# Two expert passes of at most 128 tokens with the tokens stationary and the weights streamed

## Chip, cores and metric

One core of one Trainium2 chip runs the whole program. The metric is the device time of one execution in microseconds (us). Three runs of the kernel before gave 4410.6, 4415.4 and 4421.4 us, median 4415.4 us.

## What is computed

A two-layer backbone over 1024 tokens of width 1024 (float32). The change is in the last large part, the mixture of experts of the second layer. Each token goes to 2 of 8 experts:

```python
def _moe_swiglu(h, w_router, w_gate, w_up, w_down):
    ...
    top_val, top_idx = lax.top_k(logits, TOP_K)
    ...
    g = lax.ragged_dot(xs, w_gate, group_sizes)
    u = lax.ragged_dot(xs, w_up, group_sizes)
    y = lax.ragged_dot(jax.nn.silu(g) * u, w_down, group_sizes)
    y = y * weights.reshape(-1)[order][:, None].astype(y.dtype)
    out = jax.ops.segment_sum(y, token_of, num_segments=n)
```

and the layer adds `mx[5] * _moe_swiglu(...)` to its stream, where `mx[5]` is a vector of 1024 numbers, the layer's gate. Gate and up weights are 1024 x 3584 per expert, down weights 3584 x 1024. How many tokens an expert gets is known only on the chip.

## The kernel before

The tokens of an expert are packed into passes of at most 512 (`TOKENS`). There are nine passes in this input. A table on the chip holds each pass's expert and its width class, one of `WIDTHS` (128, 160, 256, 288, ... 512). Every engine reads that table and branches to code for that width (`each_width`). So a pass of at most 128 tokens runs `one_pass(p, 128, True)`.

A pass walks over `C` = 14 chunks of 256 hidden features (`CHUNK_FF`). Float32 products are made from two fp32r parts each: a rounded part ("hi") and the rest ("lo"), with the products hi x hi, hi x lo and lo x hi. Per chunk:

- SP loads 1 MB of gate, 1 MB of up and 1 MB of down weights, into one buffer each (`raw_g`, `raw_u`, `raw_d`). A buffer is loaded again once its rest has been formed. SP's order is gate, up, down of the chunk before (`load_in`, L1807 and L1810; `load_down`, L1816).
- ACT (ScalarE) rounds each to its hi tile (`round_up`, L1985). DVE (VectorE) forms the rest of gate and up (`rest`, L2100). POOL (GpSimd) forms the rest of down (`rest_d`, L1847). Hi and lo tiles are double, one for even and one for odd chunks.
- PE (TensorE) has weights stationary and tokens moving. In a narrow pass (128 or 160 tokens) hi and lo tokens lie side by side as one moving operand of 256 or 320 columns (`product`, L1894 and L1895). `hidden` makes 32 products a chunk (2 blocks of 128 features, gate and up, 8 blocks of the input width), `down` makes 16, each of two matmuls: 96 matmuls a chunk.
- DVE adds the two halves of each sum (L2109). ACT applies SiLU (L2010). DVE multiplies by up (L2133), ACT rounds (L2017), DVE forms the rest (L2140). That gives the moving operand of `down`.
- `down` writes each of 8 blocks of the output width to one of four banks. DVE scales by the gate column and adds it to a sum in SBUF (L2149, L2153), and PE waits for a bank to be read (`y_added`) before it writes it again.

PE's order in step c is hidden(c), then down(c-1). At the end of a pass the sum is turned by PE (L1953), copied (L2056, L2221) and stored (L2060). The tokens of the next pass are turned by PE (L1883), scaled and rounded by ACT (L2029, L2032) and split by DVE (L2159) before the next pass's first `hidden`. With the last `down`, the turns of the next tokens are placed ahead of its wait for the rest of the weights. ACT's `Silu` and its `Copy` at the head of a loop body come with a table load (`ACT_TABLE_LOAD`) in every second chunk, since loop bodies hold two chunks (`chunk_pairs`).

A vector of the modulation is summed in `modulation_rest_phase`. It makes each vector in `rows` by two ones-matmuls (L851): four vectors, of which three are stored in memory. Those in `columns` are made as columns (L855). The dense layer (`ffn`) uses the same `expert_mlp_phase` at 512 tokens, with no table.

Of the kernel before, what the change touches and what calls it, by code (L numbers as in the profile page):

```python
# [792 lines left out]
def modulation_rest_phase(nc, b_ada, w_out, dram, keep):  # L793
# [7 lines left out]
    with ctx:  # L801
# [5 lines left out]
        rows = [i for i, (layer, vec) in enumerate(REST_VECTORS) if vec < 3]  # L807
# [838 lines left out]
def expert_mlp_phase(nc, name, shape, weights, columns, ident, rows_of, y_rows, table, prepare=None):  # L1646
# [590 lines left out]
def backbone(nc, a, tables, out):  # L2237
    F, R, I = mybir.dt.float32, mybir.dt.float32r, mybir.dt.int32
    dram = dict(tables)
    for name, shape, dtype in (("pool_mod", [3, D], F), ("x1", [SEQ, D], F), ("x3", [SEQ, D], F), ("xn", [SEQ, D], F),  # L2240
                               ("y_dense", [SEQ, D], F), ("y", [SLOT_TILES * P, D], F), ("slot_token", [LISTED_TILES * P, 1], I)):
        dram[name] = nc.dram_tensor(f"scratch_{name}", shape, dtype).ap()
    outer = ExitStack()
    with outer:
# [69 lines left out]
        def slot_tile(pool, p, t, to):  # L2314
# [37 lines left out]
```

## Time and profile before

| | |
|---|---|
| median of 3 runs | 4415.4 us |
| the profiled execution | 4412.7 us |
| its span (first to last instruction) | 4410.9 us |
| PE busy | 3861.9 us (88%) |
| DVE busy | 2323.4 us (53%) |
| ACT busy | 1755.2 us (40%) |
| POOL busy | 826.3 us (19%) |
| instructions | 65249 |
| mean granted TensorE clock | 0.933 of full |

Busy shares are over the whole span, and the expert part alone is about 2600 us of it, from 1784 us on. What the change is worth has to be read in the stretches of the passes that it touches.

### The profile page before, as it was taken

The numbers are of one execution on the slowest core, as the hardware profiler recorded it, in microseconds if no ns is written. First come the engines' busy times: TensorE is split into PE (matmuls) and PEld (weight loads), VectorE is DVE, ScalarE is ACT, GpSimd is POOL, SyncE is SP. The second block draws the span as 40 slices with busy tenths as digits, with TensorE's granted clock in tenths as the row PEclk, the third lists the DMA queues.
The fourth block names the chain that finished last, engine by engine and source line by source line (L and its number), as shares of the span: only waits on it lengthen the run. The fifth ranks groups of instructions, "written<-read, shape, count | busy, mean of one in ns | idle before, by whom it ended". The sixth has DMA issues, their size and how long they took to land. (4 is left out here: it accounts for less than half of the span.)

```text
span 4410.9 us, 65249 instructions
## 1 busy us (share of the span) xinstructions
PE 3861.9 (88%) x23414; PEld 3521.9 (80%) x23415; DVE 2323.4 (53%) x3372; ACT 1755.2 (40%) x2324; POOL 826.3 (19%) x319
## 2 busy tenths in 40 slices
PE   5998867999999762698999989988899998998993
PEld 3974445877877651688999989988899998998993
DVE  2338733454545452586654444448654487544555
ACT  5146613322322131555443333335533355443443
POOL 0000001111111121332222122213221233222222
PEclk8989878999999986899999999999999999999997
DMA  5136634323332233675553434346544366444554
GB/s 169 38 125 240 229 94 172 105 95 95 105 95 86 78 132 90 201 232 183 185 169 133 143 132 149 126 144 231 196 144 143 129 219 210 156 149 146 175 167 186
DMA packets 433192, 661.23 MB, mean 150 GB/s; under 512 B 33361, under 2 KB 348881, under 8 KB 432977
## 3 DMA queue, kind: packets, MB, share of 16 engines
q1 hardware_dynamic: 413026, 587.84, 40.0%
q0 software_dynamic: 15776, 55.61, 3.6%
q10 hardware_dynamic: 4176, 15.21, 0.9%
q8 instruction: 100, 1.64, 0.2%
q14 instruction: 114, 0.93, 0.1%
HBM read 599.32 MB, written 59.29 MB: 149 GB/s over the span
## 5 line engine op out<-in xcount | busy, mean ns | idle before, releaser
L1847 POOL TENSOR_TENSOR moe_d_lo<-moe_raw_d,moe_d_hi 128x2048 fp32r<-128x2048 f32 x126 | 582.8, 4625 | 1823.0 <-ACT moe_d_hi L1985 1823.0
L2153 DVE SCALAR_TENSOR_TENSOR moe_y_t<-moe_y,moe_cols,moe_y_t 128x256 f32<-128x256 f32 (+3 forms) x936 | 482.2, 534 | 185.5 <-PE moe_y L1898 176.9
L1896 PE MATMUL moe_g<-moe_x,moe_g_hi 128*128 128x352 f32 (+3 forms) x1344 | 421.2, 313 | 36.6 <-issue 36.3
L2100 DVE TENSOR_TENSOR moe_g_lo<-moe_raw_g,moe_g_hi 128x2048 fp32r<-128x2048 f32 x127 | 360.9, 2842 | 135.6 <-ACT moe_g_hi L1985 134.3
L1897 PE MATMUL moe_g<-moe_x,moe_g_hi 128*128 128x352 f32 (+3 forms) x1344 | 420.6, 313 | 0.0
L1896 PE MATMUL moe_y<-moe_h,moe_d_hi 128*128 128x352 f32 (+3 forms) x1344 | 417.9, 311 | 2.1 <-DVE moe_y_t L2153 1.1
L1898 PE MATMUL moe_g<-moe_x,moe_g_lo 128*128 128x352 f32 (+3 forms) x1344 | 419.2, 312 | 0.0
L1897 PE MATMUL moe_u<-moe_x,moe_u_hi 128*128 128x352 f32 (+3 forms) x1344 | 416.1, 310 | 0.0
L1897 PE MATMUL moe_y<-moe_h,moe_d_hi 128*128 128x352 f32 (+3 forms) x1344 | 416.0, 310 | 0.0
L1896 PE MATMUL moe_u<-moe_x,moe_u_hi 128*128 128x352 f32 (+3 forms) x1344 | 415.3, 309 | 0.0
L1898 PE MATMUL moe_u<-moe_x,moe_u_lo 128*128 128x352 f32 (+3 forms) x1344 | 415.0, 309 | 0.0
L1898 PE MATMUL moe_y<-moe_h,moe_d_lo 128*128 128x352 f32 (+3 forms) x1344 | 414.9, 309 | 0.0
L2133 DVE TENSOR_TENSOR moe_h_full<-moe_h_full,moe_u 128x352 f32<-128x352 f32 (+3 forms) x168 | 81.8, 487 | 582.2 <-PE moe_u L1898 582.1
L2017 ACT ACTIVATE moe_h<-moe_h_full 128x352 fp32r<-128x352 f32 (+5 forms) x252 | 106.0, 421 | 640.6 <-DVE moe_h_full L2133 640.6
L2100 DVE TENSOR_TENSOR moe_u_lo<-moe_raw_u,moe_u_hi 128x2048 fp32r<-128x2048 f32 x127 | 290.1, 2285 | 9.1 <-ACT moe_u_hi L1985 9.1
L1896 PEld LDWEIGHTS moe_g<-moe_x,moe_g_hi 128*128 128x128 f32 x1344 | 257.4, 191 | 38.9 <-issue 38.3
L2010 ACT ACTIVATE moe_h_full<-moe_g 128x352 f32<-128x352 f32 (+3 forms) x168 | 73.2, 436 | 526.8 <-PE moe_g L1898 526.7
L1898 PEld LDWEIGHTS moe_g<-moe_x,moe_g_lo 128*128 128x128 f32 x1344 | 258.2, 192 | 0.0
L1897 PEld LDWEIGHTS moe_g<-moe_x,moe_g_hi 128*128 128x128 f32 x1344 | 257.7, 192 | 0.0
L1985 ACT ACTIVATE moe_g_hi<-moe_raw_g 128x2048 fp32r<-128x2048 f32 x127 | 242.2, 1907 | 38.9 <-DMA moe_raw_g<-in_moe_w_gate 38.2
L1896 PEld LDWEIGHTS moe_y<-moe_h,moe_d_hi 128*128 128x128 f32 x1344 | 253.1, 188 | 3.4 <-DVE moe_y_t L2153 2.4
L1898 PEld LDWEIGHTS moe_u<-moe_x,moe_u_lo 128*128 128x128 f32 x1344 | 254.3, 189 | 0.0
(317 smaller groups left out, 9504.4 us busy)
## 6 DMA issues: line engine op xcount, KB each, us to landing
moe_raw_g<-in_moe_w_gate SPq DMA_DIRECT2D x127, 1024.0 KB, 5.6
moe_raw_u<-in_moe_w_up SPq DMA_DIRECT2D x127, 1024.0 KB, 5.0
moe_raw_d<-in_moe_w_down SPq DMA_DIRECT2D x126, 1024.0 KB, 4.9
att_w_mod<-in_w_ada SPq DMA_DIRECT2D x20, 2048.0 KB, 8.5
scratch_y<-att_zeros SPq DMA_DIRECT2D x11, 2048.0 KB, 13.8
ffn_raw_g<-in_ffn_w_gate SPq DMA_DIRECT2D x22, 1024.0 KB, 5.4
ffn_raw_u<-in_ffn_w_up SPq DMA_DIRECT2D x22, 1024.0 KB, 5.4
ffn_raw_d<-in_ffn_w_down SPq DMA_DIRECT2D x22, 1024.0 KB, 4.8
```

The source lines that it names most:

```text
L1847: pool.tensor_tensor(d_lo[par][:, :, :], raw_d[:, :, :], d_hi[par][:, :, :].bitcast(F), ALU.subtract)\
L1896: pe.matmul(bank[:, 0:width], wh, moving[:, 0, 0:width], start=start, stop=False)
L1897: pe.matmul(bank[:, 0:width], wh, moving[:, 1, 0:width], start=False, stop=False)
L1898: return pe.matmul(bank[:, 0:width], wl, moving[:, 0, 0:width], start=False, stop=stop)
L1985: act.activation(hi[par][:, :, :], raw[:, :, :], ACT.Copy).then_inc(rounded, 1)
L2010: act.activation(h_full[:, f, 0:width], gate, ACT.Silu).then_inc(silu_done, 1)
L2017: act.activation(h[par][:, f, 0, 0:width], h_full[:, f, 0:width], ACT.Copy).then_inc(h_rounded, 1)
L2100: dve.tensor_tensor(lo[par][:, :, :], raw[:, :, :], hi[par][:, :, :].bitcast(F), ALU.subtract).then_inc(split, 1)
L2133: dve.tensor_tensor(h_full[:, f, 0:width], h_full[:, f, 0:width], up, ALU.mult)\
L2153: dve.scalar_tensor_tensor(y_t[:, db, 0:cols], y_ps[db % 4][:, 0:cols], gate, y_t[:, db, 0:cols], ALU.mult, ALU.add).then_inc(y_added, 1)
```

## The change

For a pass of width class 128 of the expert part, and for no other, each engine now runs `pass_of_few` in place of the old body. Loads (SP), `rest_d` (POOL) and the formulas of rounding and rest stay. New in it:

- Gate and up tiles share one tile, `gu_hi` and `gu_lo`, side by side. For every pass, wide ones too, they are now written and read as 8 runs of 256 with a stride of 512.
- `hidden_few`: the tokens (128 x 128 block, hi or lo) are the stationary operand, gate and up weights stream as 512 columns. Three matmuls for each of 8 blocks of the input: 24 a chunk, into one bank.
- `silu_few`, `whole_few`: one SiLU and one product a chunk, 256 wide, in place of two of each and four sums of halves.
- `turn_few`: the result has tokens on partitions, so PE turns it back (2 transposes), between the two halves of the next chunk's `hidden_few`. ACT rounds what is turned (`round_few`), DVE forms the rest (`rest_few`).
- `down_few`: the turned hidden block is stationary, down weights stream as 512 columns: 12 matmuls a chunk, summed in two banks over all 14 chunks. The 8 sums a chunk on DVE are gone.
- At the end two multiplies by the gate as a row, and one store. The gate row comes from memory by a DMA that ACT issues at the pass's start. `modulation_rest_phase` makes that vector as a fourth stored row as well as a column. The turn of the result is gone.
- In the last chunk the turns of the next tokens come behind the wait for the rest of the down weights, where they stood ahead of it.

ACT's order in a step is: round gate (c+1), SiLU (c), round up (c+1), round hidden (c), round down (c). DVE's is: rest of gate (c+1), product (c), rest of up (c+1), rest of hidden (c).

```diff
-        rows = [i for i, (layer, vec) in enumerate(REST_VECTORS) if vec < 3]
+        rows = [i for i, (layer, vec) in enumerate(REST_VECTORS) if vec < 3 or (layer, vec) == (1, 5)]
...
+        gu_hi = [sb(f"gu_hi{i}", [P, KD, 2, CHUNK_FF], R) for i in range(2)]
+        gu_lo = [sb(f"gu_lo{i}", [P, KD, 2, CHUNK_FF], R) for i in range(2)]
+        g_hi, u_hi = ([w[:, :, side, :] for w in gu_hi] for side in range(2))
+        g_lo, u_lo = ([w[:, :, side, :] for w in gu_lo] for side in range(2))
...
+            def hidden_few(p, c, par, first, count):
+                n = p * C + c
+                early = type(c) is int and c < 2
+                if first == 0:
+                    if early and c == 0:
+                        pe.wait_ge(x_split, (p + 1) * KD + 2)
+                    pe.wait_ge(g_split, n + W0 + 1)
+                    pe.wait_ge(u_split, n + W0 + 1)
+                    if not early:
+                        pe.wait_ge(h_whole, (n - 1) * FB + H0)
+                for k in range(first, first + count):
+                    wh, wl = (w[par][:, k, :, :].rearrange("p s f -> p (s f)") for w in (gu_hi, gu_lo))
+                    bank = g_ps[par][:, :]
+                    pe.matmul(bank, x[:, k, 0, 0:P], wh, start=(k == 0), stop=False)
+                    pe.matmul(bank, x[:, k, 0, 0:P], wl, start=False, stop=False)
+                    last = pe.matmul(bank, x[:, k, 1, 0:P], wh, start=False, stop=(k == KD - 1))
+                if first + count == KD:
+                    last.then_inc(u_done, FB)
+
+            def turn_few(p, c, par):
+                n = p * C + c
+                pe.wait_ge(h_whole, (n + 1) * FB + H0)
+                if not (type(c) is int and c == 0):
+                    pe.wait_ge(h_split, (n - 1) * FB + H0)
+                for f in range(FB):
+                    last = pe.transpose(u_ps[par][:, f * P:(f + 1) * P], h_full[:, par, f * P:(f + 1) * P], ident[:, :])
+                last.then_inc(g_done, FB)
+
+            def down_few(p, c, par):
+                n = p * C + c
+                first, final = (type(c) is int and c == at for at in (0, C - 1))
+                if first:
+                    pe.wait_ge(y_left, p * TILES_PASS + O0)
+                    pe.wait_ge(y_right, p * TILES_PASS + O0)
+                pe.wait_ge(d_split, n + W0 + 1)
+                pe.wait_ge(h_split, (n + 1) * FB + H0)
+                if final:
+                    for k in range(4):
+                        turn_rows(p + 1, k)
+                for half in range(2):
+                    cols = slice(half * 512, (half + 1) * 512)
+                    for f in range(FB):
+                        if final:
+                            turn_rows(p + 1, 4 + half * FB + f)
+                        hh, hl = (h[par][:, f, i, 0:P] for i in range(2))
+                        pe.matmul(y_ps[half][:, :], hh, d_hi[par][:, f, cols], start=first and f == 0, stop=False)
+                        pe.matmul(y_ps[half][:, :], hh, d_lo[par][:, f, cols], start=False, stop=False)
+                        last = pe.matmul(y_ps[half][:, :], hl, d_hi[par][:, f, cols], start=False, stop=final and f == FB - 1)
+                last.then_inc(y_done, KD)
+
+            def pass_of_few(p):
+                def step(c, par):
+                    hidden_few(p, c, par, 0, KD // 2)
+                    turn_few(p, c - 1, 1 - par)
+                    hidden_few(p, c, par, KD // 2, KD // 2)
+                    down_few(p, c - 1, 1 - par)
...
+            def pass_of_few(p):
+                act.wait_ge(y_turned, p * KD + T0)
+                act.dma_start(gate_all, gate_row.partition_broadcast(P)).then_inc(gate_loaded, 16)
+
+                def step(c, par):
+                    round_g(p, c + 1, 1 - par)
+                    silu_few(p, c, par)
+                    round_u(p, c + 1, 1 - par)
+                    round_few(p, c, par)
+                    round_d(p, c, par)
...
+                def step(c, par):
+                    rest_g(p, c + 1, 1 - par)
+                    whole_few(p, c, par)
+                    rest_u(p, c + 1, 1 - par)
+                    rest_few(p, c, par)
...
+                for half in range(2):
+                    cols = slice(half * 512, (half + 1) * 512)
+                    last = dve.tensor_tensor(y_out[:, 0, cols], y_ps[half][:, :], gate_all[:, cols], ALU.mult)
+                last.then_inc(y_right, TILES_PASS)
```

## Rows read from the trace of the kernel before

**Rows 1.** The page's busy times, then its slices (tenths of full clock).

```profile
PE 3861.9 (88%) x23414; PEld 3521.9 (80%) x23415; DVE 2323.4 (53%) x3372; ACT 1755.2 (40%) x2324; POOL 826.3 (19%) x319
...
PEclk8989878999999986899999999999999999999997
```

**Rows 2.** Groups by line and shape, 1780 to 4411 us: busy, mean ns | idle before.

```profile
L1894 PE MATMUL moe_g<-moe_x,moe_g_hi 128*128 128x256 f32 x448 | 115.5, 293 | 13.8 <-DVE moe_x L2159 6.2 <-issue 5.7 <-DVE moe_g_lo L2100 1.9
```

**Rows 3.** Timeline of PE in one narrow chunk: start, duration in us [idle before].

```profile
1890.88 0.58 PE L1894 MATMUL moe_y<-moe_h,moe_d_hi 128*128 128x256 f32 x1 [1.89 <-DVE moe_y_t L2153]
...
1891.47 0.41 PE L1894 MATMUL moe_y<-moe_h,moe_d_hi 128*128 128x256 f32 x1
1891.68 0.41 PE L1895 MATMUL moe_y<-moe_h,moe_d_lo 128*128 128x256 f32 x1
...
1894.40 0.28 PE L1894 MATMUL moe_g<-moe_x,moe_g_hi 128*128 128x256 f32 x1
1894.52 0.28 PE L1895 MATMUL moe_g<-moe_x,moe_g_lo 128*128 128x256 f32 x1
```

**Rows 4.** Stretches: us, busy (x) of PE, PEld, DVE, ACT, POOL, PEclk, DMA share, GB/s.

```profile
1879.20:1906.40 27.20, 24.98 (x193) 24.58 (x192) 22.02 (x37) 15.93 (x17) 9.12 (x3) 0.94 0.70 233
...
1890.90:1894.30 3.40, 3.40 (x16) 3.40 (x17) 2.64 (x7) 2.44 (x2) 1.77 (x1) 0.50 0.95 317
1796.60:1802.20 5.60, 5.59 (x26) 5.60 (x27) 1.78 (x2) 5.34 (x5) 2.12 (x3) 0.50 0.73 226
```

**Rows 5.** Timeline of POOL at both ends of the two narrow passes of 128.

```profile
1810.98 4.60 POOL L1847 TENSOR_TENSOR moe_d_lo<-moe_raw_d,moe_d_hi 128x2048 fp32r<-128x2048 f32 x1 [10.51 <-ACT moe_d_hi L1985]
...
1974.45 4.62 POOL L1847 TENSOR_TENSOR moe_d_lo<-moe_raw_d,moe_d_hi 128x2048 fp32r<-128x2048 f32 x1 [8.97 <-ACT moe_d_hi L1985]
1988.06 4.54 POOL L1847 TENSOR_TENSOR moe_d_lo<-moe_raw_d,moe_d_hi 128x2048 fp32r<-128x2048 f32 x1 [9.00 <-ACT moe_d_hi L1985]
...
2977.25 4.59 POOL L1847 TENSOR_TENSOR moe_d_lo<-moe_raw_d,moe_d_hi 128x2048 fp32r<-128x2048 f32 x1 [26.05 <-ACT moe_d_hi L1985]
...
3141.22 4.60 POOL L1847 TENSOR_TENSOR moe_d_lo<-moe_raw_d,moe_d_hi 128x2048 fp32r<-128x2048 f32 x1 [8.98 <-ACT moe_d_hi L1985]
```

**Rows 6.** Timeline of POOL, then of DVE, in the pass that follows the first.

```profile
2028.69 4.65 POOL L1847 TENSOR_TENSOR moe_d_lo<-moe_raw_d,moe_d_hi 128x2048 fp32r<-128x2048 f32 x1 [21.46 <-ACT moe_d_hi L1985]
...
2030.45 5.04 DVE L2100 TENSOR_TENSOR moe_g_lo<-moe_raw_g,moe_g_hi 128x2048 fp32r<-128x2048 f32 x1 [3.19 <-ACT moe_g_hi L1985]
2035.41 0.41 DVE L2133 TENSOR_TENSOR moe_h_full<-moe_h_full,moe_u 128x256 f32<-128x256 f32 x1
2035.74 2.28 DVE L2100 TENSOR_TENSOR moe_u_lo<-moe_raw_u,moe_u_hi 128x2048 fp32r<-128x2048 f32 x1
```

**Rows 7.** Timeline of ACT: a narrow chunk, a wide one, a narrow pass's start.

```profile
1890.33 0.31 ACT L2017 ACTIVATE moe_h<-moe_h_full 128x128 fp32r<-128x128 f32 x1 [3.14 <-DVE moe_h_full L2133]
1890.55 1.90 ACT L1985 ACTIVATE moe_d_hi<-moe_raw_d 128x2048 fp32r<-128x2048 f32 x1
...
2023.27 0.40 ACT L2017 ACTIVATE moe_h<-moe_h_full 128x256 fp32r<-128x256 f32 x1
...
2964.85 1.28 ACT L1985 ACT_TABLE_LOAD   x1 [6.08 <-PE moe_u L1895]
```

**Rows 8.** Timeline of PE: 512 columns in the dense layer, and transposes.

```profile
900.04 0.39 PE L1896 MATMUL ffn_g<-ffn_x,ffn_g_hi 128*128 128x512 f32 x1
900.27 0.39 PE L1897 MATMUL ffn_g<-ffn_x,ffn_g_hi 128*128 128x512 f32 x1
...
1988.34 0.60 PE L1883 MATMUL moe_g<-ident,moe_x_rows 128*128 128x128 f32 x4
```

**Rows 9.** The page's DMA issues: count, KB each, median us to landing.

```profile
moe_raw_d<-in_moe_w_down SPq DMA_DIRECT2D x126, 1024.0 KB, 4.9
```

**Rows 10.** Timeline of PE in the modulation's rest: the ones-matmuls, rows then columns.

```profile
574.24 10.07 PE L851 MATMUL rest_row_ps<-mod_sum,rest_ones 128*128 128x512 f32 x16 [15.59 <-DMA rest_col_bias<-in_b_ada]
584.15 17.86 PE L855 MATMUL rest_col_ps<-rest_ones,mod_sum 128*128 128x1 f32 x96
```

More of the change, by code:

```diff
@@ L1643, in _, with expert_mlp_phase @@
                 norm(t)
-def expert_mlp_phase(nc, name, shape, weights, columns, ident, rows_of, y_rows, table, prepare=None):
+def expert_mlp_phase(nc, name, shape, weights, columns, ident, rows_of, y_rows, table, prepare=None, gate_row=None):
     F, R = mybir.dt.float32, mybir.dt.float32r
@@ L1714, in expert_mlp_phase, with few @@
         y_done, y_added, y_turned, y_left, y_right = (sem(n) for n in ("y_mm", "y_add", "y_t2", "y_l", "y_r"))
+        gate_loaded = sem("gate_ld") if table is not None else None
+        gate_all = y_t[:, 0:2, :].rearrange("p a b -> p (a b)")
+        def few(width):
+            return table is not None and width == P
         W0, U0, X0, H0, Y0, A0, T0, O0 = 1, 2 * FB, KD, FB, 2 * KD, 4, KD, TILES_PASS
@@ L1958, in one_pass @@
             def one_pass(p, width, narrow):
+                if few(width):
+                    pass_of_few(p)
+                    return
                 hidden(p, 0, parity(p, 0), width, narrow)
@@ L2032, in ready_tokens, with silu_few, round_few @@
                     act.activation(x[:, k, 0, :], x_full[:, k % 2, :], ACT.Copy).then_inc(x_rounded, 1)
-            def one_pass(p, width, narrow):
+            def silu_few(p, c, par):
+                act.wait_ge(u_done, (p * C + c + 1) * FB + U0)
+                act.activation(h_full[:, par, 0:CHUNK_FF], g_ps[par][:, 0:CHUNK_FF], ACT.Silu).then_inc(silu_done, FB)
+            def round_few(p, c, par):
+                n = p * C + c
+                act.wait_ge(g_done, (n + 1) * FB)
+                act.wait_ge(y_done, (n - 1) * KD + Y0)
+                act.activation(h[par][:, :, 0, 0:P], u_ps[par][:, 0:CHUNK_FF].rearrange("p (f q) -> p f q", f=FB), ACT.Copy)\
+                   .then_inc(h_rounded, FB)
+            def pass_of_few(p):
[7 more added lines that the diff above has]
+                    round_d(p, c, par)
+                chunk_pairs(act, p, 0, C - 2, step)
+                step(C - 1, parity(p, C - 1))
+                ready_tokens(p + 1)
+                act.wait_ge(y_right, (p + 1) * TILES_PASS + O0)
+                act.sem_inc(y_left, TILES_PASS)
+                act.dma_start(y_rows(p, 0), y_out[:, 0, :]).then_inc(y_stored[0], 16)
+                for t in range(1, TILES_PASS):
+                    act.wait_ge(y_stored[t % 2], (p * (TILES_PASS // 2) + t // 2 + 1) * 16)
+                    act.sem_inc(y_stored[t % 2], 16)
+            def one_pass(p, width, narrow):
+                if few(width):
+                    pass_of_few(p)
+                    return
+                if table is not None:
+                    act.sem_inc(gate_loaded, 16)
                 def step(c, par, round_next=True):
@@ L2322, in backbone @@
         expert_mlp_phase(nc, "moe", (MAX_PASSES, FF_EXPERT // CHUNK_FF), experts, keep["moe_cols"], keep["ident"], slot_tile,
-                         tile_rows(dram["y"]), keep["table"], list_slots)
+                         tile_rows(dram["y"]), keep["table"], list_slots, dram["pool_mod"][3, :])
         output_phase(nc, a["final_gain"], dram, keep, out)
```

34 lines of the change are left out of this document (29 added, 5 removed).

## The prediction

> **What bounds the kernel now.** The page first: PE is busy 88% of the span and its granted clock is mostly full [rows 1]. That is an average, so the second view is the groups by shape. The 256-column form of L1894 stands 448 times for gate, and a pass makes 14 x 16 = 224 of them, so two of the nine passes have width 128 and take the new code. Everything below is about these two and about their neighbours.
>
> Third, the beat of such a pass, read where POOL starts on each chunk's down weights. From chunk 0 to chunk 12 it is 1974.45 - 1810.98 = 163.5 us in the first and 3141.22 - 2977.25 = 164.0 us in the second, mean 163.7, which is 13.64 us a chunk [rows 5]. PE's own work is less: 96 matmuls, 0.12 us from start to start [rows 3], are 11.5 us. The rest is a stall of 1.89 us in `down`, where PE waits for DVE's sum into `y_t` [rows 3], and a stretch at half clock behind it: two chunks have a mean clock of 0.94, the 3.4 us behind the stall 0.50 [rows 4]. DVE has 22.0 us of work in 27.2, ACT 15.9, POOL 9.1, and the DMA share is 0.70 [rows 4]. So the pass is bound by PE and DVE together, and the others are not far off. The engine that gets faster here is PE. The question is what the order of the other engines allows.
>
> **PE's work.** 512 columns take 0.227 us from start to start (900.04 to 900.27) [rows 8]. 24 + 12 matmuls are 8.2 us, two transposes 0.3: 8.5 us against 11.5. Taken alone that is 3 us a chunk. DVE loses eight sums and four halvings. Neither sets the end, if a loop of waits is longer.
>
> **The loop of waits.** In the new order PE turns hidden block c in the middle of hidden(c+1). From there everything hangs in one chain back to the next turn. Counted from the start of turn(c):
>
> - two transposes: four last 0.60 with 0.11 between starts, so two last 0.38 [rows 8];
> - ACT rounds the turned block: 0.03 to start, 0.40 [rows 7];
> - ACT rounds the down weights right behind, 1.90, with a start 0.09 before the last one's end (1890.55 against 1890.64) [rows 7];
> - POOL forms their rest: 0.08 to start, 4.6 [rows 5];
> - meanwhile ACT rounds gate(c+2), and DVE is to form its rest. Both inputs of that lie in SBUF, as POOL's do. The trace has the case: POOL ran 2028.69 to 2033.34, DVE started L2100 at 2030.45 and took 5.04 instead of 2.28. It ended 2.15 after POOL did, so it hardly moved while POOL ran [rows 6]. In the new order POOL always starts ahead of it, 1.9 us of gate rounding before. So the rest of gate ends 2.15 after POOL;
> - product(c+1), behind it on DVE: 0.41, of which 0.33 adds (2035.41 to 2035.74) [rows 6];
> - rest of up(c+2): 2.28, of which 2.20 adds [rows 6]. ACT has the rounding of up ready by then, even with the two table loads of 1.28 [rows 7] of every second chunk: 0.72 + 1.8 + 1.28 + 1.9 + 1.28 + 0.4 + 1.85 = 9.2 us against the 9.8 at which DVE gets to it;
> - PE starts hidden(c+2) some 0.1 later, and 12 matmuls, 2.72 us, bring it to turn(c+1).
>
> Sum: 0.38 + 0.43 + 1.81 + 4.70 + 2.15 + 0.33 + 2.20 + 0.10 + 2.72 = 14.8 us. That is more than the 13.64 of now. `down`(c) stands on a side branch. It starts 0.2 behind POOL's end, at 7.5, and has until 12.1.
>
> **The clock.** PE is idle from the end of hidden(c+1), about 3.1, to 7.5. After the 1.89 us stall the trace has 3.4 us at 1.2 GHz [rows 3, 4], where 256 columns take 0.21 us [rows 3] and 512 so twice that, 0.427. After 6.2 us of idling before a pass [rows 2] the first 5.6 us were at that level [rows 4]. The low stretch will fall on `down`: 8 matmuls at 0.427 and 4 at 0.227 are 4.3 us, which ends at 11.8 and costs nothing. If it lasts 5.6, `down` ends at 12.7 and 1 us of hidden's half is slow: 1.1 us more. I take 0.25, nearer the 3.4 that repeats in the pass, and so 15.05 us a chunk. Ends for the range: 14.8 and 15.9.
>
> A rule of the Trainium skill speaks against the change here: "TensorE: Matmul & The Clock Gate", section "HAM oscillation — how this bites in real kernels", tells of a product of 128 rows whose bursts between waits each start at the low clock, and advises loops that keep PE fed. By it each chunk pays for one burst. By my chain that burst is `down` and costs 0 to 0.25 us; were every burst slow, it would be the third rival's time. The trace of before agrees in kind: one 1.89 us gap in two chunks is followed by 3.4 us at 0.50 [rows 3, 4].
>
> **The ends of a pass.** The first chunk has no overlap. Before, POOL ended chunk 0 at 1815.6. Now hidden(0) from 1796.6 has 5.6 us at half clock [rows 4], 13 matmuls, and 11 at full: to 1804.6 and 0.2 to drain. SiLU 0.4, up 1.8, rest 2.3: 1809.3. Half of hidden(1), slow at first, 4.3; turn, block, down weights, POOL 0.4 + 0.4 + 1.9 + 4.7: 1821.0, 5.4 us later. In the second pass ACT starts at 2964.85 [rows 7], plus 0.4 for issuing the gate row (a DMA issue; no row has this one, bounds 0 to 1): 1.3 + 1.9 + 1.3 + 0.4 + 1.8 + 2.3 brings rest of up to 2974.3, then the same 4.3 + 7.4 to 2986.0, against 2977.25 + 4.6 = 2981.85: 4.2 later. Mean 4.8.
> Chunk 12 to 13 took 1988.06 - 1974.45 = 13.6 [rows 5]. Now `down`(12) 0.2 + 4.3, turn(13) 0.4, block 0.4, down weights 1.8, POOL 4.7: 11.8, so -1.8.
> Hand-over to the next pass: the turns of its tokens start behind POOL and not before it, up to 4.6 later, but the sums, the turn of the result and its copies go. I take 0, between -3 and +4.
>
> **Around it.** The fourth stored row costs two ones-matmuls of 512 columns. Four records a vector, 10.07 / 16 each, are 2.5 us, and the columns' matmuls follow without a gap [rows 10], so PE ends that phase later by it: +2.5, with 0.1 for one more load. Strided hi and lo tiles change no count of elements: 0, bounds -1 and +8 us over all passes; the wide passes are bound by PE and would hide it. The gate row is read 13 chunks after it is asked for: 0. Removed instructions of PE's sequencer: 0.
>
> **The sum.** Per pass 4.8 + (12 x 15.05 - 163.7) - 1.8 + 0 = 4.8 + 16.9 - 1.8 = 19.9. Two passes 39.8, with 2.6 for the row: +42.4. The profiled execution took 4412.7, so 4455.1. The median of the three runs stands 2.7 above it: 4458, rounded to 4457. What a measurement can tell from no change is 0.3%, 13 us.
>
> **Rivals.**
> 1. The beat falls to the loop of the down buffer, and the kernel gets faster. POOL's end, 0.2 to the DMA issue, 4.9 to land [rows 9], 1.9 + 0.1 on ACT, 4.6 on POOL: 11.7, say 12.0. This needs ACT, DVE and PE never to wait for each other in the order above. 12 x 12.0 - 163.7 = -19.7; with 4.8 - 1.8, -16.7 a pass, -31 in all: 4384. It decides from a beat below 13.3 us, where the ends and the row are paid (24 x 0.36 = 8.6). For it: the 0.70 DMA share leaves room. Against it: the turn in mid-chunk ties ACT's down rounding to PE.
> 2. DVE isn't held by POOL. Then the rest of gate is done by 7, and the chain runs over ACT alone or over `down`. In chunks with table loads 0.38 + 0.43 + 1.8 + 1.3 + 1.9 + 1.3 + 0.4 + 1.85 + 2.28 + 0.1 + 2.72 = 14.5. In the others POOL, `down` and half of hidden: 0.4 + 0.4 + 1.8 + 4.7 + 0.2 + 2.7 to 4.3 + 2.7 = 12.9 to 14.5. Mean about 14.1: 12 x 14.1 - 163.7 = +5.5, +8.5 a pass, +20 in all: 4435. For it: DVE's sums with a PSUM input aren't slowed in the trace. Against it: the 5.04 us row.
> 3. The clock stays low in every burst. `down` 12 x 0.427 = 5.1 and half of hidden 5.1: 0.5 + 0.4 + 1.8 + 4.7 + 0.2 + 5.1 + 5.1 = 17.8. 12 x 17.8 - 163.7 = +49.9, +53 a pass, +109 in all: 4524. For it: PE is to be busy 8.5 of 15 us. Against it: in the pass now the clock came back within 3.4 us each time, with the same kind of gap.
> 4. The new code isn't taken. Excluded by the 448 [rows 2].
>
> **How the numbers follow.** Forecast (beat 14.8 to 15.9, ends and strides within their bounds, 4440 to 4485) 0.72; first rival 0.07; second 0.11; third 0.10. The range of 4424 to 4495 takes in the second rival and the half of the third's way in which part of hidden's half is slow. Slower by over 0.3% is the forecast, the third and nearly all of the second: 0.88. Within 0.3%: the ends between the second and the first, 0.07. Faster: 0.05.
>
> **What the profile will show.** Starts of POOL's L1847 some 15 us apart in two passes. DVE's rest of gate at 3.6 to 5 us there, ending 2.1 after POOL. PE waiting for POOL before `down` by over 3 us each chunk, then slow matmuls in `down` and full ones in hidden. The 512-column matmuls 0.227 apart. PE's busy time lower by some 70 us, and the time longer for all that. The prediction is wrong if the beat is under 13.6, if rest of gate runs at 2.3 us, or if the wide passes change their beat.

## The result and the profile after

The changed kernel took 4468.4 us (median of 4 runs, 4462.6 to 4473.1), the kernel before 4418.4 us beside it. The ratio is 1.0113, with an interval of 1.0089 to 1.0136: slower by 50 us. The forecast was 4457 us with a range of 4424 to 4495. The profiled execution took 4465.0 us, with a span of 4463.2 us against 4410.9.

Of the page of after, the line of busy times, the granted clock in 40 slices, and the group of DVE's rests of gate:

```profile
PE 3830.9 (86%) x21778; PEld 3415.4 (77%) x21779; DVE 2206.2 (49%) x2982; ACT 1738.8 (39%) x2266; POOL 823.6 (18%) x319
PEclk8988878999999986789999999998799999999996
L2217 DVE TENSOR_TENSOR moe_gu_lo<-moe_raw_g,moe_gu_hi 128x2048 fp32r<-128x2048 f32 x127 | 388.9, 3063 | 222.1 <-ACT moe_gu_hi L2062 220.8
```

Every engine has less to do than in [rows 1], and the time is longer. A slice is 111.6 us. In slices 17 and 18 (1785 to 2008 us) the clock is 7 and 8 where the kernel before has 8 and 9, in slices 28 and 29 (3013 to 3236 us) 8 and 7 where it has 9 and 9: the two narrow passes. The page can say no more than that.

POOL's starts on the down weights, from the timeline of after (start, duration, instruction, idle time before it and what ended it), chunks 0, 1, 12 and 13 of the first narrow pass:

```profile
1830.56 4.51 POOL L1854 TENSOR_TENSOR moe_d_lo<-moe_raw_d,moe_d_hi 128x2048 fp32r<-128x2048 f32 x1 [16.48 <-ACT moe_d_hi L2062]
1846.02 4.50 POOL L1854 TENSOR_TENSOR moe_d_lo<-moe_raw_d,moe_d_hi 128x2048 fp32r<-128x2048 f32 x1 [10.95 <-ACT moe_d_hi L2062]
...
2014.49 4.52 POOL L1854 TENSOR_TENSOR moe_d_lo<-moe_raw_d,moe_d_hi 128x2048 fp32r<-128x2048 f32 x1 [10.62 <-ACT moe_d_hi L2062]
2027.32 4.49 POOL L1854 TENSOR_TENSOR moe_d_lo<-moe_raw_d,moe_d_hi 128x2048 fp32r<-128x2048 f32 x1 [8.31 <-ACT moe_d_hi L2062]
```

(2014.49 - 1830.56) / 12 is 15.33 us a chunk. The second narrow pass gives 15.31 in the same way. Before it was 13.64 [rows 5]. From chunk 12 to 13 it is 12.8 us here and 11.8 in the other pass, where before it was 13.6.

Two chunks out of the middle of that pass, from the timeline of after, all engines, in the order of the chain and not of time:

```profile
1904.44 0.38 PE L1992 MATMUL moe_u<-ident,moe_h_full 128*128 128x128 f32 x2
1904.99 0.39 ACT L2121 ACTIVATE moe_h<-moe_u 128x256 fp32r<-128x256 f32 x1 [9.51 <-PE moe_u L1992]
1905.27 1.91 ACT L2062 ACTIVATE moe_d_hi<-moe_raw_d 128x2048 fp32r<-128x2048 f32 x1
1907.26 4.50 POOL L1854 TENSOR_TENSOR moe_d_lo<-moe_raw_d,moe_d_hi 128x2048 fp32r<-128x2048 f32 x1 [11.04 <-ACT moe_d_hi L2062]
1910.43 3.48 DVE L2217 TENSOR_TENSOR moe_gu_lo<-moe_raw_g,moe_gu_hi 128x2048 fp32r<-128x2048 f32 x1 [4.40 <-ACT moe_gu_hi L2062]
1913.84 0.41 DVE L2284 TENSOR_TENSOR moe_h_full<-moe_h_full,moe_g 128x256 f32<-128x256 f32 x1
1914.17 2.28 DVE L2217 TENSOR_TENSOR moe_gu_lo<-moe_raw_u,moe_gu_hi 128x2048 fp32r<-128x2048 f32 x1
1911.82 0.63 PE L2013 MATMUL moe_y<-moe_d_hi,moe_h 128*128 128x512 f32 x1 [4.22 <-POOL moe_d_lo L1854]
...
1915.57 0.40 PE L2013 MATMUL moe_y<-moe_d_hi,moe_h 128*128 128x512 f32 x1
1916.69 0.50 PE L1979 MATMUL moe_g<-moe_gu_hi,moe_x 128*128 128x512 f32 x1 [0.26 <-DVE moe_gu_lo L2217]
1919.57 0.38 PE L1992 MATMUL moe_u<-ident,moe_h_full 128*128 128x128 f32 x2
...
1922.41 4.52 POOL L1854 TENSOR_TENSOR moe_d_lo<-moe_raw_d,moe_d_hi 128x2048 fp32r<-128x2048 f32 x1 [10.65 <-ACT moe_d_hi L2062]
1926.98 0.80 PE L2013 MATMUL moe_y<-moe_d_hi,moe_h 128*128 128x512 f32 x1 [4.25 <-POOL moe_d_lo L1854]
...
1931.84 0.63 PE L2015 MATMUL moe_y<-moe_d_hi,moe_h 128*128 128x512 f32 x1
1932.27 0.51 PE L1979 MATMUL moe_g<-moe_gu_hi,moe_x 128*128 128x512 f32 x1
1935.15 0.38 PE L1992 MATMUL moe_u<-ident,moe_h_full 128*128 128x128 f32 x2
```

What to see: the turn of the hidden block at 1904.44 leads to the block's rounding, the rounding of down, POOL, then DVE's rest of gate. That ends at 1913.91, 2.15 after POOL's end (1911.76), although POOL's work has nothing to do with it. Product, rest of up, half of `hidden`, and the next turn at 1919.57: 15.13 us. In the second chunk rest of up would have let `hidden` go earlier. But all 12 matmuls of `down` run at the low level of TensorE's clock (0.43 from start to start, 1926.98 to 1932.27; the granted clock there is 0.50), and PE gets to `hidden` late: 15.58 us from turn to turn. The two alternate through the pass.

Where the 52.3 us of span went, from the two traces:

| stretch | before | after | difference |
|---|---|---|---|
| start to last matmul of attention | 558.7 | 569.5 | +10.8 |
| from there to the last matmul of the routing (the added row lies here) | 1160.5 | 1161.1 | +0.6 |
| from there to the first matmul of the expert part | 64.4 | 66.6 | +2.2 |
| first to last matmul of the expert part | 2559.3 | 2599.1 | +39.8 |
| from there to the end | 68.0 | 66.9 | -1.1 |

The fourth row was forecast as +39.8. The first has the same code in both kernels, and is treated below.

### The profile page after: what moved, and what is told of

Same layout as the page of the kernel before. It is cut to its first block and busy times, and to the rows that moved or that the text cites. A ratio compares the mean times of both kernels' runs of the same rounds, so it can differ in the third digit from the quotient of the medians.

```text
span 4463.2 us, 60571 instructions
## 1 busy us (share of the span) xinstructions
PE 3830.9 (86%) x21778; PEld 3415.4 (77%) x21779; DVE 2206.2 (49%) x2982; ACT 1738.8 (39%) x2266; POOL 823.6 (18%) x319
## 5 line engine op out<-in xcount | busy, mean ns | idle before, releaser
L2217 DVE TENSOR_TENSOR moe_gu_lo<-moe_raw_g,moe_gu_hi 128x2048 fp32r<-128x2048 f32 x127 | 388.9, 3063 | 222.1 <-ACT moe_gu_hi L2062 220.8
L2270 DVE SCALAR_TENSOR_TENSOR moe_y_t<-moe_y,moe_cols,moe_y_t 128x352 f32<-128x352 f32 (+3 forms) x728 | 392.5, 549 | 176.8 <-PE moe_y L1905 176.1
L1903 PE MATMUL moe_g<-moe_x,moe_gu_hi 128*128 128x352 f32 (+3 forms) x1344 | 421.5, 314 | 35.7 <-issue 25.4
L1904 PE MATMUL moe_g<-moe_x,moe_gu_hi 128*128 128x352 f32 (+3 forms) x1344 | 420.4, 313 | 0.0
L1905 PE MATMUL moe_g<-moe_x,moe_gu_lo 128*128 128x352 f32 (+3 forms) x1344 | 420.3, 313 | 0.0
L1905 PE MATMUL moe_u<-moe_x,moe_gu_lo 128*128 128x352 f32 (+3 forms) x1344 | 415.7, 309 | 0.0
L1903 PE MATMUL moe_u<-moe_x,moe_gu_hi 128*128 128x352 f32 (+3 forms) x1344 | 415.3, 309 | 0.3 <-DVE moe_gu_lo L2217 0.3
L1904 PE MATMUL moe_u<-moe_x,moe_gu_hi 128*128 128x352 f32 (+3 forms) x1344 | 415.3, 309 | 0.0
L2217 DVE TENSOR_TENSOR moe_gu_lo<-moe_raw_u,moe_gu_hi 128x2048 fp32r<-128x2048 f32 x127 | 290.0, 2283 | 13.9 <-ACT moe_gu_hi L2062 13.9
L1903 PEld LDWEIGHTS moe_g<-moe_x,moe_gu_hi 128*128 128x128 f32 x1344 | 258.6, 192 | 38.1 <-issue 36.7
L1904 PEld LDWEIGHTS moe_g<-moe_x,moe_gu_hi 128*128 128x128 f32 x1344 | 258.2, 192 | 0.0
L1905 PEld LDWEIGHTS moe_g<-moe_x,moe_gu_lo 128*128 128x128 f32 x1344 | 258.0, 192 | 0.0
L1903 PEld LDWEIGHTS moe_u<-moe_x,moe_gu_hi 128*128 128x128 f32 x1344 | 253.9, 189 | 0.5 <-DVE moe_gu_lo L2217 0.5
## 6 DMA issues: line engine op xcount, KB each, us to landing
scratch_y<-att_zeros SPq DMA_DIRECT2D x11, 2048.0 KB, 13.6
```

What stands on the lines that cost most here:

```text
L1903: pe.matmul(bank[:, 0:width], wh, moving[:, 0, 0:width], start=start, stop=False)
L1904: pe.matmul(bank[:, 0:width], wh, moving[:, 1, 0:width], start=False, stop=False)
L1905: return pe.matmul(bank[:, 0:width], wl, moving[:, 0, 0:width], start=False, stop=stop)
L2217: dve.tensor_tensor(lo[par][:, :, :], raw[:, :, :], hi[par][:, :, :].bitcast(F), ALU.subtract).then_inc(split, 1)
L2270: dve.scalar_tensor_tensor(y_t[:, db, 0:cols], y_ps[db % 4][:, 0:cols], gate, y_t[:, db, 0:cols], ALU.mult, ALU.add).then_inc(y_added, 1)
```

## The experiments

Names begin with x where one cause is tested, with b where a better version was sought, with r for repeats. A ratio is always to the kernel before, run on the same chip. Differences between edited kernels are differences of medians, some of them from different chips, on which the kernel before had medians of 4418 to 4424 us; a few us in them mean nothing.

### The two kernels again

`r_after` is the changed kernel without an edit:

> The changed kernel once more, unedited. Of its 52 us over the kernel before, in the profiled executions, 39 lie in the expert part and 13 ahead of it: 11 of these in the attention phase, which the diff doesn't touch. Theory (chance of the execution): attention ends anywhere within some 10 us from execution to execution, here not at 569.5 again, and the two passes' beat stays 15.3 us. Rival (the change of memory layout costs the attention phase 11 us): it ends at 569 to 570 again. Time by both about 4468, ratio 1.009 to 1.013.

It took 4469.5 us, ratio 1.0123 (1.01 to 1.0147), with 15.38 and 15.40 us a chunk. `r_before` is the kernel before without an edit:

> The kernel before once more, unedited, for its attention phase. In ten profiled executions of nine kernels, whose code is the same up to there but for the layout of one small tensor, the phase ended between 558.6 and 570.9 us. Theory (chance of the execution): it ends anywhere in that span. Rival (the layout): 558 to 560 as in the first profile. The beat of the passes of 128 stays 13.65 us.

It took 4411.7 us in one run, 13.60 and 13.66 us a chunk. In its trace attention ended at 564.9 us.

### Everything of the change but the new pass

```diff
         def few(width):
-            return table is not None and width == P
+            return False
```

> The changed kernel with the new passes switched off, so that passes of 128 take the old code; the shared gate-and-up tiles (stride 512) and the fourth stored row stay. Theory: these cost nothing but the row's 2.6 us, so 4418 + 3 = 4421, beat of the passes of 128 is 13.65 again, of the wide ones 17.3 and 23.0 to 23.2 as before, ratio 1.000 to 1.001. Rival (strided tiles or the row slow something): above 4429, ratio above 1.0025, with a longer beat of wide passes or a longer attention phase.

4427.4 us, ratio 1.0018 (1.0007 to 1.003), with 13.72 and 13.62 us a chunk. So the loss is in the new pass: its code is worth 4468 - 4427 = 41 us of the 50. The shared tiles and the fourth row together cost 8 us by the medians, more than the 2.6 of the sum. The trace puts 1.9 us of these at the row (attention's last matmul to the end of that phase, 45.1 against 43.3 and 43.1 in two executions of before) and 4.0 between routing and expert part (68.4 against 64.4 and 63.9), where POOL waits for the DMAs of the scattered token numbers. In the eleven executions with shared tiles that stretch is 66.6 to 71.9 us; why was not found. The stride itself costs nothing that can be seen. The three wide passes between the narrow ones, from their first rest of down to that of the second narrow pass, take 944.9 to 957.6 us in ten executions with shared tiles and the new pass, 948.6 and 952.1 in the old kernel, and 958.5 in this one.

### The turn ahead of hidden

```diff
                 def step(c, par):
-                    hidden_few(p, c, par, 0, KD // 2)
                     turn_few(p, c - 1, 1 - par)
-                    hidden_few(p, c, par, KD // 2, KD // 2)
+                    hidden_few(p, c, par, 0, KD)
                     down_few(p, c - 1, 1 - par)
```

> One step moved: the transposes of hidden block c-1 stand ahead of hidden(c), not in its middle. Nothing else changes. Theory (the chain turn, block, down weights, POOL, held rest of gate, product, rest of up, half of hidden): the last two terms and the wait for them drop out of the loop, which shrinks from 15.3 to about 10; then the loop of the single down buffer (load 4.9, round 1.9, POOL 4.6, some 0.5 between) binds at 12.0 to 12.7 us. 26 chunks by 3: 78 us less than the changed kernel, 4385 to 4400, faster than both. Rival (the beat is set by PE's half clock or by the rate of the loads): the beat stays above 14.3 and the time above 4440.

4376.3 us, ratio 0.9915 (0.9889 to 0.9942), 12.24 us a chunk. One step moved, and the loss of 50 us is a gain of 43. The 24 beats, shorter by 3.1 us each, are 74 of the 92 us between the two kernels. Another 8 or so are in the first pass's start: POOL begins 25.8 us behind the expert part's first matmul, where it was 33.4. Its timeline, again along the chain (SPq: the issue of a load):

```profile
1908.78 0.37 SPq L1823 DMA_DIRECT2D moe_raw_d<-in_moe_w_down  x1
1911.71 0.38 PE L1992 MATMUL moe_u<-ident,moe_h_full 128*128 128x128 f32 x2
1913.83 1.91 ACT L2061 ACTIVATE moe_d_hi<-moe_raw_d 128x2048 fp32r<-128x2048 f32 x1 [0.85 <-DMA moe_raw_d<-in_moe_w_down]
1915.82 4.59 POOL L1854 TENSOR_TENSOR moe_d_lo<-moe_raw_d,moe_d_hi 128x2048 fp32r<-128x2048 f32 x1 [7.27 <-ACT moe_d_hi L2061]
1920.63 0.37 SPq L1823 DMA_DIRECT2D moe_raw_d<-in_moe_w_down  x1
...
1915.28 0.49 PE L1979 MATMUL moe_g<-moe_gu_hi,moe_x 128*128 128x512 f32 x1 [3.19 <-DVE moe_gu_lo L2216]
1917.95 0.63 PE L1981 MATMUL moe_g<-moe_gu_hi,moe_x 128*128 128x512 f32 x1
1922.49 0.39 PE L2013 MATMUL moe_y<-moe_d_hi,moe_h 128*128 128x512 f32 x1
```

In this chunk the rounding of down waits no longer for PE but for its own load: 1908.78 to 1920.63, 11.85 us from issue to issue. That is the loop of the first rival (11.7, taken as 12.0). It binds in nearly half of the chunks (12 of 28 roundings wait for their load). In the others the rounding follows the turn without that wait, and PE's and ACT's own order is as long: 12.0 to 13.2 us from POOL start to POOL start. The first rival's point of decision is right too, since 12.24 is below the 13.3 from which the kernel gets faster. What made the rival false for the change itself was the place of one step.

### DVE held by POOL

In narrow passes the rest of down is formed for a quarter of the columns only, so POOL is done in 1.3 us. The rest of its tile is set to zero once; the output leaves out that much of the low parts.

```diff
+            def rest_quarter(p, c, par):
+                n = p * C + c
+                pool.wait_ge(d_rounded, n + 1)
+                pool.tensor_tensor(d_lo[par][:, :, 0:D // 4], raw_d[:, :, 0:D // 4], d_hi[par][:, :, 0:D // 4].bitcast(F), ALU.subtract)\
+                    .then_inc(d_split, 1)
```

> The changed kernel, in whose two passes of 128 POOL forms the rest of a quarter of the down weights (256 of 1024 columns); the other columns' rest is left at zero, or at what an earlier pass left. This part of the computation is left out. Theory (POOL's 4.6 us and the held rest of gate are in the loop): POOL takes some 1.2 us, the rest of gate 2.3 in each chunk and not 3.5 to 5; then ACT's chain is late next: 12.6 us in chunks without table loads, 14.7 with the two of 1.28, mean 13.6, and 24 by 1.7 = 41 us less than 4469: 4428. Rival (DVE isn't held by POOL, the 3.5 to 5 us come from the strided tiles): the rest of gate stays above 3.4 us. Rival 2 (POOL isn't in the loop): beat stays at 15.1 to 15.6.

4458.5 us, ratio 1.0085 (1.0068 to 1.0102). Only 10 us were gained where 40 were expected, and the beat stayed as long: 16.8 and 14.1 in turn. The hold itself went as expected. From its timeline:

```profile
1908.17 1.26 POOL L1864 TENSOR_TENSOR moe_d_lo<-moe_raw_d,moe_d_hi 128x512 fp32r<-128x512 f32 x1 [12.78 <-ACT moe_d_hi L2079]
1911.36 2.29 DVE L2234 TENSOR_TENSOR moe_gu_lo<-moe_raw_g,moe_gu_hi 128x2048 fp32r<-128x2048 f32 x1 [4.41 <-ACT moe_gu_hi L2079]
1909.49 0.50 PE L2030 MATMUL moe_y<-moe_d_hi,moe_h 128*128 128x512 f32 x1 [0.98 <-POOL moe_d_lo L1864]
...
1917.39 0.79 PE L1996 MATMUL moe_g<-moe_gu_hi,moe_x 128*128 128x512 f32 x1 [4.88 <-DVE moe_gu_lo L2234]
1920.97 0.57 PE L1998 MATMUL moe_g<-moe_gu_hi,moe_x 128*128 128x512 f32 x1
1922.08 0.38 PE L2009 MATMUL moe_u<-ident,moe_h_full 128*128 128x128 f32 x2
```

The rest of gate takes 2.29 us in each chunk, where it took 3.5 and 4.9. `down` starts early and runs at full speed. But with POOL's wait gone, PE's idle time moved to the place before `hidden`: 4.88 us there, and the first half of `hidden` takes 4.7 us (1917.39 to 1922.08) where it took 2.88. That half lies in the loop of waits. `down` does not. So it looks as if what was to be gained was given back by the clock. A repeat with filling matmuls behind `down`, to hold the clock up, tests that:

```diff
                 last.then_inc(y_done, KD)
+                if not first and not final:
+                    for i in range(18 if par else 9):
+                        pe.matmul(y_ps[2][:, :], x[:, 0, 0, 0:P], x[:, 1, 0, :], start=True, stop=True)
```

> As the kernel in which POOL forms a quarter of the down weights' rest (the other columns' rest is left out), with 9 or 18 filling matmuls of 512 columns behind each down, where PE waited 2.5 and 4.9 us for the rest of up and then ran the first half of hidden at half clock. Theory (the 1.7 us that the shorter POOL step should have saved went into the half clock): first halves of hidden take 2.9 us, beats 12.8 and 14.9, mean 13.9, about 36 us less than the 4458 without the filling: 4422. Rival (another wait took the place): beats stay 14.1 and 16.8.

4423.3 us, ratio 1.0005 (0.9989 to 1.0021), 14.9 and 12.5 in turn. Of its timeline:

```profile
1919.43 0.50 PE L2030 MATMUL moe_y<-moe_d_hi,moe_h 128*128 128x512 f32 x1 [1.02 <-POOL moe_d_lo L1864]
1922.29 2.20 PE L2036 MATMUL moe_y<-moe_x 128*128 128x512 f32 x9
1924.92 0.49 PE L1996 MATMUL moe_g<-moe_gu_hi,moe_x 128*128 128x512 f32 x1 [0.43 <-DVE moe_gu_lo L2237]
```

Adding 27 useless matmuls to a pair of chunks made it 35 us faster. With the clock held, the short POOL gains 45 us against the changed kernel, as the hold of DVE had promised. This comes near the second rival's case, in which POOL does not hold DVE. It is not the same, since the rival had POOL's full 4.6 us. It gave a beat of 13.7 (the rival said 14.1) and no change clear of noise against before.

### What the low clock costs in the changed kernel itself

First, 16 filling matmuls ahead of `down`'s wait, so that `down` is at full speed:

```diff
+                if not first and not final:
+                    for i in range(FILL):
+                        pe.matmul(y_ps[2][:, :], x[:, 0, 0, 0:P], d_hi[1 - par][:, 0, 0:512], start=True, stop=True)
                 pe.wait_ge(d_split, n + W0 + 1)
```

> 16 matmuls of 512 columns into a spare bank, whose result nobody reads, fill PE's wait for POOL ahead of each down but the first and last of a pass. Theory (the half clock in down adds 0.5 us on average to a loop of 14.8): granted clock in the passes about 1.0, down takes 2.7 us and not 4.6 to 5.3, beat 14.8, 24 times 0.5 = 12 us less than the changed kernel, 4456. Rival (the clock costs nothing, since down has slack; the 0.5 is elsewhere in the loop): beat stays 15.3 and time 4468. Rival 2 (the extra work is in the way): beat above 15.3.

4496.4 us, ratio 1.0183 (1.016 to 1.0205), 16.45 us a chunk: 28 us slower than the changed kernel, where a gain of 12 was expected. Of its timeline:

```profile
1923.70 0.49 PE L1980 MATMUL moe_g<-moe_gu_hi,moe_x 128*128 128x512 f32 x1 [1.84 <-DVE moe_gu_lo L2221]
...
1927.30 0.63 PE L1982 MATMUL moe_g<-moe_gu_hi,moe_x 128*128 128x512 f32 x1
1927.72 0.63 PE L1993 MATMUL moe_u<-ident,moe_h_full 128*128 128x128 f32 x2
1931.14 3.79 PE L2005 MATMUL moe_y<-moe_d_hi,moe_x 128*128 128x512 f32 x16
1935.48 0.50 PE L2017 MATMUL moe_y<-moe_d_hi,moe_h 128*128 128x512 f32 x1 [0.55 <-POOL moe_d_lo L1855]
```

`down` is fast now and ends early, which leaves 1.84 us of idle time ahead of `hidden`. In nine chunks of twelve (those of 16.6 to 16.8 us) that is enough: the half of `hidden` takes 4.0 us (1923.70 to 1927.72) in place of 2.88. The low stretch was not removed but moved, out of slack and into the loop. With 8 more matmuls behind `down`:

```diff
                 last.then_inc(y_done, KD)
+                if not first and not final:
+                    for i in range(FILL // 2):
+                        pe.matmul(y_ps[2][:, :], x[:, 0, 0, 0:P], d_hi[1 - par][:, 0, 0:512], start=True, stop=True)
```

> As the kernel with 16 filling matmuls ahead of down, and 8 more behind it, so that PE has no wait of more than about 0.5 us in a chunk. In the first the low clock had moved from down, which has slack, to the first half of hidden, which has none. Theory (a slow first half of hidden costs 1.6 us, a fast one leaves the loop at 14.9 to 15.2): granted clock about 1.0 in the passes, each 12 matmuls of the first half in 2.7 to 2.9 us, beat 14.9 to 15.2, time 4455 to 4470. Rival (the filling matmuls themselves delay hidden): beat above 15.6 with full clock.

4467.8 us, ratio 1.0113 (1.0096 to 1.013), a steady 15.2 us a chunk. From its timeline:

```profile
1904.34 0.50 PE L2017 MATMUL moe_y<-moe_d_hi,moe_h 128*128 128x512 f32 x1 [0.70 <-POOL moe_d_lo L1855]
1907.19 1.98 PE L2023 MATMUL moe_y<-moe_d_hi,moe_x 128*128 128x512 f32 x8
1909.21 0.49 PE L1980 MATMUL moe_g<-moe_gu_hi,moe_x 128*128 128x512 f32 x1
...
1919.57 0.50 PE L2017 MATMUL moe_y<-moe_d_hi,moe_h 128*128 128x512 f32 x1 [0.73 <-POOL moe_d_lo L1855]
```

Here no matmul of a chunk is at the low level, and the beat is 15.23 (1904.34 to 1919.57). So of the 15.35 us the clock is 0.1, and the loop of waits is the rest. Away from the ends of a pass, all of the low clock in the changed kernel falls on `down`, where there is slack for most of it: a `down` with 12 slow matmuls makes its chunk 0.45 us longer than one with 8 or 9 (15.58 against 15.13).

### The rest of down on DVE

In narrow passes DVE forms the rest of down, behind its rest of hidden, and POOL only fetches tokens:

```diff
+                dve.wait_ge(d_rounded, p * C + c + 1)
+                dve.tensor_tensor(d_lo[par][:, :, :], raw_d[:, :, :], d_hi[par][:, :, :].bitcast(F), ALU.subtract)\
+                    .then_inc(d_split, 1)
```

> The changed kernel with the rest of the down weights formed by DVE, right behind the rest of the hidden block, and not by POOL, in the two passes of 128 alone. All work is done. Theory: DVE needs 2.28 us where POOL took 4.5, and nothing holds the rest of gate any more. Loop from turn to turn: without table loads 0.55 + 0.39 + 1.81 + 0.05 + 2.28 + 2.2 + 0.33 + 2.2 + 0.25 + 2.8 = 12.8; with them ACT is late, 14.7. Mean 13.7, beat 1.6 less, 38 us less: 4431. Rival (a busier DVE is late: it gets 2.3 us more work in 15): beat stays above 15.

4455.5 us, ratio 1.0076 (1.0059 to 1.0093), 15.07 us a chunk. The step of 4.5 us on POOL became one of 2.29 on DVE, and the beat fell by 0.3. Expected was 13.7. It looks like the same miss as above, from its timeline:

```profile
1914.71 0.79 PE L1983 MATMUL moe_g<-moe_gu_hi,moe_x 128*128 128x512 f32 x1 [3.88 <-DVE moe_gu_lo L2221]
1915.29 0.63 PE L1984 MATMUL moe_g<-moe_gu_lo,moe_x 128*128 128x512 f32 x1
...
1919.99 0.45 PE L1996 MATMUL moe_u<-ident,moe_h_full 128*128 128x128 f32 x2
```

Here are 3.88 us of idle time ahead of `hidden`, and its half takes 5.28 us (1914.71 to 1919.99). That the clock took the rest of the gain wasn't tested in this kernel by filling. Both moves together, the turn first and the rest of down on DVE:

> Both steps: turn ahead of hidden, and the rest of the down weights on DVE. Turn first alone gave 4376 with a beat of 12.24, where two loops are equally long: the down buffer (0.2 + 4.9 + 1.9 + 4.7 = 11.8) and hidden 5.7 (7.4 where the clock is half) + SiLU 0.4 + up 1.8 + its rest 2.2 + 0.3. Theory: the buffer's loop falls to 9.5, and PE's gap shrinks so that its clock falls less often; hidden's loop is left, 10.4 without and 11.7 with a table load that stands behind the wait for hidden: beat 11.0 to 11.8, time 4350 to 4366. Rival (hidden's loop is as long as before, since the clock still falls): beat 12.2, time 4376. Rival 2 (the loads' rate, 3.1 MB a chunk): beat above 12 with a DMA share near 1.

4367.9 us, ratio 0.9888 (0.9864 to 0.9912), 12.13 us a chunk where 11.0 to 11.8 was expected. Idle time ahead of `hidden` is 3.19 us in one such chunk, with low clock behind it. So, at last, filling matmuls between the turn and `hidden`:

```diff
                     turn_few(p, c - 1, 1 - par)
-                    hidden_few(p, c, par, KD // 2, KD // 2)
+                    if not (type(c) is int and c == 1):
+                        for i in range(12 if par else 8):
+                            pe.matmul(y_ps[2][:, :], x[:, 0, 0, 0:P], x[:, 1, 0, :], start=True, stop=True)
+                    hidden_few(p, c, par, 0, KD)
```

> Turn first and the rest of the down weights on DVE, as in the 4368 us version, with 8 or 12 filling matmuls between the turn and hidden, so that PE's clock doesn't fall. Theory (hidden in 7.4 us instead of 5.7 in a part of the chunks is what keeps the beat at 12.1): every hidden takes 5.7, beats 10.6 and 11.8, mean 11.2, 24 by 0.9 = 22 us less: 4346. Rival (the filling delays hidden, or the loads bind): beat 12 or more, 4365 or more.

4359.0 us, ratio 0.9859 (0.983 to 0.9888), 11.32 us a chunk: 109 us faster than the changed kernel and 1.4% faster than the one before. Of its timeline:

```profile
1911.61 0.39 PE L2017 MATMUL moe_y<-moe_d_hi,moe_h 128*128 128x512 f32 x1
1914.33 0.38 PE L1996 MATMUL moe_u<-ident,moe_h_full 128*128 128x128 f32 x2
1914.47 2.99 PE L2027 MATMUL moe_y<-moe_x 128*128 128x512 f32 x12
1917.90 0.49 PE L1983 MATMUL moe_g<-moe_gu_hi,moe_x 128*128 128x512 f32 x1 [0.44 <-DVE moe_gu_lo L2223]
1911.85 1.28 ACT L2120 ACT_TABLE_LOAD   x1 [2.12 <-PE moe_g L1985]
```

PE is idle for 0.44 us in this chunk, every matmul is 0.227 behind the one before, and there is no wait left ahead of `down`. The time is 13 us above the 4346 expected. The beat accounts for 3 of these (24 x 0.12). Against the profiled execution of `b_dve_down` the 24 beats are 19 us shorter, but the wide passes, whose code is the same, are 14 us longer: 950.4 us against 944.9 between the two narrow passes, and 1143.4 against 1134.7 from the first rest of down behind the second one to the last matmul. The latter stretch is 1145.2 and 1138.6 us in the two executions of the old kernel. So wide passes differ by that much between executions, and the beat says more of the filling than the 9 us between the medians.

## Why the prediction was right, and where it was not

**The loop of waits** was right, and each term can be read in the rows above. Turn and block's rounding: 1904.44 to 1905.27 is 0.83 (0.81 forecast). Down's rounding to POOL's end: 6.49 (6.51). The held rest: 2.15 (2.15). Product and rest of up: 1913.91 to 1916.45 is 2.54 (2.53). To the next turn: 3.12 (2.82). Together 15.13 against 14.8. That `x_turn_first`, which takes the last of these terms out of the loop, has a beat of 12.24 shows that this loop set the beat. The term that was mis-sized is the last. The half of `hidden` takes 2.88 and not 2.72, since the first matmul behind a wait is 0.34 from the next and not 0.227, and the wait's end costs 0.24 and not 0.10.

**The hold of DVE by POOL** rested on one row of a wide pass [rows 6]. It is shown: 2.15 us behind POOL's end with a long POOL, 2.29 us in all with a short one. The Trainium skill ("SBUF — State Buffer", section "Who interferes with whom") tells of such contention between a VectorE instruction with two SBUF inputs and GpSimd, and this trace agrees.

**The clock** was right in size, 0.25 a chunk forecast and some 0.2 measured (15.35 less 15.13, or 0.1 by `x_fill_both`), but the picture of it was too simple. The forecast had 8 slow matmuls in each `down`. They are 8 or 9 in one chunk and all 12 in the next, and there `hidden` starts 0.66 us after the end of the rest of up and not 0.24. The larger lesson is what the prediction did not see. The low clock was cheap only since PE's longest wait stood ahead of work with slack. Of the gains expected of shortening that wait, most did not come: 10 us of 41 in `x_pool_quarter`, 13 of 38 in `x_dve_down`, and a loss of 28 for a gain of 12 in `x_fill`, each time with a slow half of `hidden`. The second rival was priced at 4435 with full speed in `hidden`. The nearest to it that was run, with an even shorter POOL step, gives 4458 without filling matmuls. The Trainium skill ("TensorE: Matmul & The Clock Gate", section "HAM oscillation — how this bites in real kernels") advises to restructure such loops so that PE stays at the high clock. The 35 us gained by useless matmuls in `x_quarter_fill` agree with it. `x_fill` shows the limit: with PE fed in one place only, the kernel was 28 us slower.

**PE's work** was forecast to fall by 70 us and fell by 31. The 8.5 us a chunk held for full clock, though the forecast's own paragraph on the clock had `down` at 4.3 us and not 2.7. With 4.6 to 5.3 us in `down`, PE is busy 110.2 us between 1845 and 1999 us, 11.0 a chunk against 11.9 before, by the view of stretches:

```profile
1845.00:1999.00 154.00, 110.22 (x384) 83.86 (x384) 71.62 (x41) 75.17 (x61) 45.11 (x10) 0.83 0.62 205
```

The columns are those of [rows 4]: the clock is 0.83 where it was 0.94. The term changed nothing in the sum.

**The ends of a pass.** First POOL start behind the first `hidden`: 20.3 us (1810.24 to 1830.56) against 14.4, so +5.9 where 5.4 was forecast. In the second pass it is 23.7 (2993.48 to 3017.15) against 18.1 (2959.15 to 2977.25), +5.6 where 4.2 was forecast; the two repeats give +3.9. Chunk 12 to 13: -0.8 and -1.8, forecast -1.8. Hand-over: -2.0 and -1.5, taken as 0. With 20.5 and 19.8 for the twelve beats the first pass comes to +23.6 and the second to about +22, 46 in all where 39.8 was forecast. That the expert part as a whole shows 39.8 is luck: its wide passes happen to be 6 us shorter in this execution, within their scatter.

**Around it.** The added row was priced at 2.6 us, from 10.07 us for 16 records. From the groups by shape of after, 560 to 640 us:

```profile
L851 PE MATMUL rest_row_ps<-mod_sum,rest_ones 128*128 128x512 f32 x20 | 11.3, 733 | 16.5 <-DMA rest_col_bias<-in_b_ada 16.5
```

Four records more are 11.3 - 10.07 = 1.2 us: the records overlap, and a share of their time is not the cost of one more. The phase as a whole is 1.1 us longer in the profiled execution, and 0.4 to 2.0 in the others, most of it in the loads ahead of its first matmul.

**What the sum does not hold** are the 10.8 us of attention. Its code is the same in all kernels here. In 13 executions its end lies between 558.6 and 570.9 us: 558.7 and 564.9 in the kernel before, 569.5 and 565.8 in the changed one, 559.2 in `x_fill_both`. In one stretch of it, 360 to 560 us, the mean granted clock is 0.89 before and 0.85 after. So the clock takes a different course in it from execution to execution. That the changed kernels lie later on the average (567 in ten, 561 in three with the old passes) may be chance or not. What could make it so is open. The medians differ by 50 us, of which the new pass has 41 (to `x_no_few`), the row and the stretch behind routing 3 to 6. The rest is within what executions of one kernel differ by, which is 10 us and more here. So the forecast of 4457 came near the measured 4468 with the right mechanism, but some of the closeness in its parts is chance. (Its sum comes to 4457.8, which it writes as 4457.)

**The rivals.** The first (4384) was a good price for another order: 4376 measured with the turn ahead. The second fell, by the 3.5 to 4.9 us of the rest of gate. The third fell as well: from the third chunk of a pass on, the half of `hidden` ahead of the turn takes 2.7 to 2.9 us. It is slow only in the second chunk (4.4 and 5.3 us in the two passes), which the forecast had at 4.3. That the code is not taken was excluded.

## What to carry to other kernels

Before an engine is made faster, close the loop of waits in the new order of instructions, with one duration from the trace for each step; here it gave 14.8 us for 15.1 to 15.6 measured, while the engine's own work said the opposite. Where a result must be turned or handed on in mid-loop, try that step ahead of the next block of work and not in its middle: here 2.9 us of matmuls stood in the loop for nothing, and moving one step was worth 92 us. When a wait of TensorE is shortened or moved, ask which work comes behind the wait that is then the longest, since in `x_pool_quarter`, `x_dve_down` and `x_fill` that was the work that ran at the low clock.

## What was not expected of the hardware

- A gap of 1.84 us ahead of `hidden` was followed by low clock (`x_fill`, 1923.70), and one of 1.86 us in the same place one chunk later (1940.36) by none. The clock's course depends on more than the last gap.
- In the changed kernel the chunks of 15.1 and 15.6 us alternate. In the profiled execution the odd ones are short in the first narrow pass and the even ones in the second, in the same code. The table loads stand in the same chunks of both. So it is not they that make a chunk long, but how much of `down` runs at the low clock: in `x_fill_both`, at full clock, the alternation is gone.
- A table load that ACT reaches early waits with the SiLU behind it for PE: in `b_fill` it begins at 1911.85 after 2.12 us of idle time, so its 1.28 us lies in the path there. In the changed kernel it ran ahead, unnoticed.
